# A two-layer sequence model on one core: half of the first input projection cut along its contraction and set between the loads of the first modulation

## The chip, the core and the metric

The kernel runs as one program on one core of a Trainium2 chip. The core has five engines with their own instruction streams: TensorE (PE: matmuls, and PEld: the loading of the stationary operand), VectorE (DVE), ScalarE (ACT), GpSimd (POOL) and SyncE (SP, which here only issues DMA transfers). They wait for each other through semaphores. All data are float32. The metric is the time of one execution on the device in microseconds, less is better. The kernel before takes 3230.65 us, the median of three runs from 3228.79 to 3232.77.

## The reference, cut to what matters

Two blocks with 256 tokens of width 2048 are computed one after the other. The change touches only the very start of the first block, its first layer:

```
c_act = silu(c)                                         # one vector of 2048
shift, scale, gate = split(c_act @ mod_w[0] + mod_b[0])  # 2048 x 6144
h = rmsnorm(x, norm_g[0]) * (1 + scale) + shift          # 256 x 2048
u, z = split(h @ w_in, 2)                                # 2048 x 4096, u and z 256 x 2048 each
dt = exp(log_step); a = exp(lam * dt)                    # the state space model's constants
bb = coefficient(a, lam) * b
x = scan(a, u * bb); y = gelu(Re(c * x) + d * u)          # the S5 scan along the 256 tokens
y = y * sigmoid(y @ w_glu + b_glu)
out = (y * silu(z)) @ w_out
```

After it come a sparse attention layer and a whole second model; nothing of their work is changed.

## The kernel before, in words

Weights stream from HBM in tiles of 2 MB. A tile is 128 partitions by 4096 floats: 16 chunks (`j`) along the contraction by 256 output columns. Four such tiles have room on the chip at once, in `ring`, whose four slots are filled in turn: tile number n lies in slot n % 4. SP issues the loads strictly in order, and `load` (L208 to L211) waits with each until its slot has been handed back (`slot_free`). One DMA queue carries all of them. Activations lie transposed, width on the partitions: `xT` and `hT` hold 16 chunks by 256 tokens, 2 MB each.

The start runs in these steps:

- SP loads the constants, `xT` and the raw state space matrices, then the 16 tiles of `mod0` (shift and scale of the first layer), then small parameters, then the tiles of `u`, among which are mixed the tiles for later modulations (`stream_mixed`).
- DVE computes the constants of the state space model (`dve_ssm_params`, `dve_ssm_matrices`: 18 large operations on 128x2048 floats), and then waits for the modulation.
- For each of the 16 tiles of `mod0`, PE multiplies the vector `c_act` with the tile (`mod_rows`, L388), ACT copies the resulting row to `ROW_STAGE` and hands the slot back (L972), and PE turns the row into columns (`mod_row_columns`, L394), one tile later, while the next tile's rows are done. From the ninth tile on, PE also does two blocks of transposes per tile for the state space model (`pe_transposed`, L1145 and L1150), and ACT copies them away.
- When all 32 columns are there, DVE adds the bias and forms `hT` in four quarters of 4 chunks each (`dve_norm0`, L979 to L993), and signals `h_ready` after each.
- PE does the first input projection `u` (`dense`, L280): eight tiles of 256 output columns, each 2 x 16 matmuls of 128x128 by 128x256. The profile counts each float32 matmul as two records, so a tile has 64. ACT drains each tile's bank into `u_all` (L414).
- Beside it DVE forms four pairs of modulation tiles (`mod_pair`, L348 and L350: one pair of tiles, weighted by `c_act` and summed over the 16 chunks), and PE sums each over the partitions (`mod_columns`, L365).
- Then comes the scan (`pe_ssm`, `dve_ssm`, `act_ssm`, `pool_ssm`), 16 blocks, with the tiles of `z` worked off between them.

The order of the instructions on each engine is written out by hand; there is no scheduler. Every engine takes its stream in order.

## Time and profile before

| | us |
|---|---|
| three runs, median | 3230.65 |
| the profiled execution's own time | 3228.36 |
| span in its profile | 3226.6 |
| PE busy in the span | 3142.2 (97%) |
| first rows of the first modulation tile, start | 26.47 |
| last rows of the sixteenth, start | 101.20 |
| first matmul of `u`, start | 110.06 |
| last `mod_columns` beside `u`, end | 226.8 |

The profile is of one execution. Its times count from the span's start. A chain of waits goes back from the last instruction to what released each step. A stretch's row gives each engine's busy time in it, and the granted clock of PE (1.00 is 2.4 GHz, 0.50 is 1.2 GHz). PE is busy nearly all the time, but not in the first 120 us, and that is where the change lies.

### The profile page before, as it was taken

What the parts mean: (1) busy time and instruction counts of PE and PEld (TensorE: products, weight loads), DVE (VectorE), ACT (ScalarE), POOL (GpSimd) and SP (SyncE); (2) the same over time, 40 slices, a digit from 0 to 9 for tenths busy, and PEclk for the clock granted to TensorE, in tenths of its full rate; (3) what the DMA queues carried; (4) which work ended last, traced back from release to release, by engine and by line L of the source; (5) the groups of instructions that cost most, each with busy time, mean ns of one, the idle gap of its engine ahead of it and who ended that gap; (6) DMA issues with size and microseconds to landing.
All of it is one profiled execution on the core that took longest, in us unless ns stands there. A gap on an engine that the chain in (4) does not pass through costs nothing.

```text
span 3226.6 us, 54024 instructions
## 1 busy us (share of the span) xinstructions
PE 3142.2 (97%) x22938; PEld 2866.8 (89%) x22938; DVE 1730.4 (54%) x2645; ACT 454.2 (14%) x801; POOL 139.3 (4%) x89
## 2 busy tenths in 40 slices
PE   5899999989999999999999999999999999999999
PEld 3788888878889888898888888899999999999999
DVE  6448844444245243475636754567665655555443
ACT  2104510000001133312310012210000000000000
POOL 0004310000000000021000000000010000000000
PEclk8999999999999999999999999999999999999999
DMA  9873568766574323243344442324544444444443
GB/s 409 339 288 158 202 253 324 291 256 245 229 287 152 136 105 130 105 153 138 128 159 168 157 144 98 133 105 147 193 157 173 166 165 173 159 179 162 161 166 137
DMA packets 51017, 599.38 MB, mean 186 GB/s; under 512 B 9535, under 2 KB 12190, under 8 KB 13342
## 3 DMA queue, kind: packets, MB, share of 16 engines
q1 hardware_dynamic: 50846, 596.88, 48.0%
q8 instruction: 134, 2.20, 0.3%
q14 instruction: 37, 0.30, 0.0%
HBM read 593.70 MB, written 3.16 MB: 185 GB/s over the span
## 4 chain that ended last, share of the span: by engine, by line
PE 93%; DMA 3%; DVE 2%; DVEq 1%; ACT 0%; issue 0%; SPq 0%; POOLq 0%; POOL 0%; ACTq 0%
PE bank L2601 25%; PE bank L735 18%; PE bank L280 16%; PE bank L786 16%; PE bank L310 4%; DMA ring<-in_t_mod 3%; PE bank L732 2%; PE bank L322 2%; PE bank L561 1%; PE aux L1609 1%; PE bank L388 1%; PE bank L551 1%; PE aux L1656 1%; PE aux L1231 1%; PE bank L518 1%; PE bank L1249 0%
## 5 line engine op out<-in xcount | busy, mean ns | idle before, releaser
L735 PE MATMUL bank<-hT,ring 128*128 128x256 f32 x2496 | 552.5, 380 | 0.0
L735 PEld LDWEIGHTS bank<-hT,ring 128*128 128x128 f32 x2496 | 470.8, 190 | 76.6 <-issue 15.3
L2601 PE MATMUL bank<-arena,ring 128*128 128x128 f32 x3440 | 396.4, 275 | 0.0
L2601 PEld LDWEIGHTS bank<-arena,ring 128*128 128x128 f32 x3440 | 390.2, 192 | 0.0
L280 PE MATMUL bank<-arena,ring 128*128 128x256 f32 x1536 | 336.6, 381 | 8.3 <-DVE arena L635 5.7
L280 PEld LDWEIGHTS bank<-arena,ring 128*128 128x128 f32 x1536 | 292.2, 191 | 49.1 <-issue 6.0
L786 PE MATMUL bank<-hT,ring 128*128 128x128 f32 x2624 | 320.2, 277 | 7.7 <-DVEq L841 5.8
L786 PEld LDWEIGHTS bank<-hT,ring 128*128 128x128 f32 x2624 | 305.6, 193 | 13.2 <-issue 7.2
L280 PE MATMUL bank<-hT,ring 128*128 128x256 f32 x1024 | 224.9, 382 | 4.8 <-DVE hT L993 4.8
L280 PEld LDWEIGHTS bank<-hT,ring 128*128 128x128 f32 x1024 | 194.8, 191 | 32.2 <-issue 4.5
L2601 PE MATMUL bank<-hT,ring 128*128 128x128 f32 x1680 | 197.9, 275 | 0.0
L2601 PEld LDWEIGHTS bank<-hT,ring 128*128 128x128 f32 x1680 | 192.7, 192 | 0.1
L350 DVE SCALAR_TENSOR_TENSOR E<-ring,c_act,E 128x512 f32<-128x512 f32 x240 | 181.7, 757 | 19.0 <-issue 1.3
L786 PE MATMUL bank<-arena,ring 128*128 128x128 f32 x1472 | 175.6, 275 | 0.0
L786 PEld LDWEIGHTS bank<-arena,ring 128*128 128x128 f32 x1472 | 170.2, 192 | 0.4
L2692 DVE TENSOR_TENSOR arena<-bank,w_gate 128x256 f32<-128x256 f32 x50 | 21.2, 424 | 204.1 <-ACT rstd L2640 132.5
L2601 PE MATMUL bank<-arena,E 128*128 128x128 f32 x1024 | 119.7, 275 | 0.0
L2601 PEld LDWEIGHTS bank<-arena,E 128*128 128x128 f32 x1024 | 117.0, 192 | 0.0
L310 PE MATMUL bank<-hT,ring 128*128 128x256 f32 x512 | 116.0, 385 | 0.0
L310 PEld LDWEIGHTS bank<-hT,ring 128*128 128x128 f32 x512 | 96.8, 192 | 14.8 <-issue 0.4
L2098 DVE TENSOR_TENSOR W<-E,arena 128x128 f32<-128x128 f32 (+7 forms) x64 | 74.8, 1169 | 46.7 <-issue 29.6
L1676 DVE TENSOR_TENSOR arena<-aux,con 128x60 f32<-128x60 f32 (+2 forms) x24 | 17.1, 712 | 129.7 <-PE aux L1609 129.7
(438 smaller groups left out, 3639.6 us busy)
## 6 DMA issues: line engine op xcount, KB each, us to landing
ring<-in_t_mod SPq DMA_DIRECT2D x64, 2048.0 KB, 13.4
ring<-in_t_gu SPq DMA_DIRECT2D x44, 2048.0 KB, 8.2
ring<-in_t_out SPq DMA_DIRECT2D x16, 2048.0 KB, 8.3
ring<-in_t_zs SPq DMA_DIRECT2D x16, 2048.0 KB, 8.3
ring<-in_t_down SPq DMA_DIRECT2D x16, 2048.0 KB, 7.4
ring<-in_t_gdn SPq DMA_DIRECT2D x12, 2048.0 KB, 8.2
ring<-in_t_u SPq DMA_DIRECT2D x8, 2048.0 KB, 10.3
ring<-in_t_z SPq DMA_DIRECT2D x8, 2048.0 KB, 9.1
```

Of the source, the lines that this page charges most:

```text
L280: last = nc.tensor.matmul(bank[s][:, T * f:T * f + T], w[:, j, P * f:P * f + P], act[:, j, :], start=j == 0, stop=j == kd - 1)
L310: last = nc.tensor.matmul(bank[s][:, T * f:T * f + T], w[:, j, P * f:P * f + P], act[:, j, :], start=j == 0, stop=j == KD - 1)
L322: last = nc.tensor.matmul(bank[s][:, T * f:T * f + T], act[:, j, P * f:P * f + P], w[:, j, :], start=j == 0, stop=j == KD - 1)
L350: nc.vector.scalar_tensor_tensor(a, w, c_act[:, j:j + 1], a, ALU.mult, ALU.add)
L388: last = nc.tensor.matmul(out[32 * q:32 * q + 32, :], c_act[:, j:j + 1].to_broadcast([P, 32]), w[:, j, :], start=a == 0, stop=a == KD // 4 ...
L518: last = nc.tensor.matmul(out[:, T * f:T * f + T], w[:, j, P * f:P * f + P], act[:, j, :], start=m == 0, stop=m == 2 * KD - 1)
L551: last = nc.tensor.matmul(out[:, T * f:T * f + T], w[:, j, P * f:P * f + P], x[:, j, :], start=j == 0 and f == 0, stop=j == KD - 1 and f == 1)
L732: last = nc.tensor.matmul(out[:, T * f:T * f + T], act[:, j, P * f:P * f + P], w[:, j, :], start=j == 0, stop=j == kd - 1)
L735: last = nc.tensor.matmul(out[:, T * f:T * f + T], w[:, j, P * f:P * f + P], act[:, j, :], start=j == 0, stop=j == kd - 1)
L786: last = nc.tensor.matmul(out[:, P * at:P * at + P], a[:, j, :], tile_at(b, j), start=j == 0 and q in (0, 3), stop=j == half - 1 and q in ...
L2098: v.tensor_tensor(tmp, Tsol[:, :, 0:J], row, ALU.mult)
L2601: last = nc.tensor.matmul(out[:, P * q:P * q + P], a[:, j, :], b[:, j, :], start=begins and q == 0 and j == 0, stop=ends and q == len(grou ...
```

## The change

The projection `u` (2048 columns out of 2048) is cut in two halves of 1024 output columns.

The first half is cut along the contraction: four tiles `uk`, each with 4 chunks of the contraction (one quarter of `hT`) by 1024 output columns, again 2 MB. They take places in the stream of `mod0`, which is reordered: after four modulation tiles that give shift and scale of one quarter comes that quarter's `uk` tile. So `mod0` has 20 tiles. PE works each off in `pe_u_slice` (32 matmuls, into four banks that are kept open over all four slices), after `h_ready` for its quarter. DVE forms `hT` quarter by quarter as the columns come: the first quarter in the midst of `dve_ssm_matrices`, the others behind it. The transposes for the state space model move into the second and third slice, one block of them after each group of four matmuls, and through one bank of `aux` in place of two banks. `mod_rows` now writes to `aux`, and the columns of a tile follow its rows at once, after ACT's copy.

The second half is done as before in four tiles of 256 columns (`pe_u_rest`), but the weights go to two side rooms in place of ring slots: `arena[:, 4096:8192]`, free when the transposes are done (`k0_ready`), and `xT`, free when `hT` is complete. The pairs of modulation tiles have the ring alone: pair 0 in slots 0 and 1, pair 1 in 2 and 3, and so on. For that the raw matrices lie in the arena and no longer in `hT`, a rounding buffer of the scan lies in `w_gate`, and `w_gate` itself is loaded after the scan, ahead of the second load of `xT`.

```
-ORDER = [("mod0", 16), ("u", 16), ("z", 16), ("glu", 16), ("out", 16), ("kv", 16), ("kvrow", 4),
+ORDER = [("mod0", 20), ("u", 8), ("z", 16), ("glu", 16), ("out", 16), ("kv", 16), ("kvrow", 4),
...
+        def mod0_slot(m):
+
+            q, x = m // QUARTER, m % QUARTER
+            return 5 * q + x, 8 * (x // 2) + 2 * q + x % 2
+
+        def whole(name, k):
+            return (lambda slot: slot[:, 0:SLOT]), t["t_" + name][k]
+
+        def stream_mod0(sp):
+            for q in range(4):
+                for m in range(QUARTER * q, QUARTER * q + QUARTER):
+                    n, tile = mod0_slot(m)
+                    load(sp, n, 0, whole("mod", tile))
+                load(sp, 5 * q + 4, 0, whole("uk", q))
+
+        U_ROOMS = [arena[:, 4096:8192], xT[:].rearrange("p j n -> p (j n)")]
+        u_in = [sem(f"u_in{q}") for q in range(2)]
+        u_drained = sem("u_drained")
+
+        def sp_u_rest(sp):
+
+            def dense_load(m):
+                if m == 0:
+                    sp.wait_ge(k0_ready, 1)
+                elif m == 1:
+                    sp.wait_ge(h_ready, 4)
+                else:
+                    sp.wait_ge(products, 4 + m - 1)
+                sp.dma_start(U_ROOMS[m % 2], t["t_u"][m]).then_inc(u_in[m % 2], 16)
+
+            def pair_load(p):
+                for x, (n, r) in enumerate(mod_slots("u", p // 2, p % 2)):
+                    load(sp, n, r, whole("mod", 2 * PAIRS["u"] + 2 * p + x))
+
+            dense_load(0)
+            pair_load(0)
+            dense_load(1)
+            pair_load(1)
+            for p in (2, 3):
+                dense_load(p)
+                pair_load(p)
...
+        def pe_u_slice(pe, q):
+
+            n = 5 * q + 4
+            wait_landed(pe, n, 0)
+            pe.wait_ge(h_ready, q + 1)
+            w = ring[:, n % RING, :].rearrange("p (j n) -> p j n", j=QUARTER)
+            for o in range(8):
+                for j in range(QUARTER):
+                    last = nc.tensor.matmul(bank[o // 2][:, T * (o % 2):T * (o % 2) + T], w[:, j, P * o:P * o + P],
+                                            hT[:, QUARTER * q + j, :], start=q == 0 and j == 0 and o % 2 == 0,
+                                            stop=q == 3 and j == QUARTER - 1 and o % 2 == 1)
+                if q == 3 and o % 2:
+                    last.then_inc(products, 1)
+                elif q < 3 and o == 7:
+                    last.then_inc(slot_free[n % RING], 1)
+                if q in TURNED:
+                    pe_transposed(pe, 8 * TURNED.index(q) + o)
+
+        def pe_u_rest(pe):
+            for m in range(4):
+                pe.wait_ge(u_in[m % 2], 16 * (m // 2 + 1))
+                pe.wait_ge(u_drained, m + 1)
+                w = U_ROOMS[m % 2].rearrange("p (j n) -> p j n", n=SLOT_COLS)
+                for f in range(2):
+                    for j in range(KD):
+                        last = nc.tensor.matmul(bank[m][:, T * f:T * f + T], w[:, j, P * f:P * f + P], hT[:, j, :],
+                                                start=j == 0, stop=j == KD - 1)
+                last.then_inc(products, 1)
+                if m:
+                    mod_columns(pe, "u", (m - 1) // 2, (m - 1) % 2)
+            mod_columns(pe, "u", 1, 1)
+
+        def act_u(act, first):
+            for m in range(first, first + 4):
+                act.wait_ge(products, m + 1)
+                if m == 3:
+                    act.nop().then_inc(slot_free[(BASE["u"] - 1) % RING], 1)
+                act.wait_ge(params_in, 16 * N_PARAMS)
+                nc.scalar.activation(u_all[:, 2 * m:2 * m + 2, :], bank[m % 4][:].rearrange("p (f n) -> p f n", f=2),
+                                     ACT.Copy).then_inc(u_drained, 1)
...
-            for n in range(COUNT["mod0"]):
-                if n > 1:
-                    wait_free(pe, n + RING - 2, 0)
-                wait_landed(pe, n, 0)
-                mod_rows(n, bank[n % 2][:, 0:SLOT_COLS])
-                if n:
-                    wait_free(pe, n + RING - 1, 0)
-                    mod_row_columns(ROW_STAGE[(n - 1) % 2], A(1, 2 * n - 2, 2))
-                if n >= FIRST_TURNED:
-                    for b in range(2):
-                        pe_transposed(pe, 2 * (n - FIRST_TURNED) + b)
-            wait_free(pe, n + RING, 0)
-            mod_row_columns(ROW_STAGE[n % 2], A(1, 2 * n, 2))
+
+            def columns(m):
+                n, tile = mod0_slot(m)
+                wait_free(pe, n + RING, 0)
+                mod_row_columns(ROW_STAGE[m % 2], A(1, 2 * tile, 2))
+
+            for q in range(4):
+                for m in range(QUARTER * q, QUARTER * q + QUARTER):
+                    n, _ = mod0_slot(m)
+                    wait_landed(pe, n, 0)
+                    mod_rows(n, MOD_ROWS)
+                    columns(m)
+                pe_u_slice(pe, q)
 
             pe.wait_ge(bT_kept, SBLOCKS)
 
         def act_mod0(act):
...
+            for q in range(4):
+                for m in range(QUARTER * q, QUARTER * q + QUARTER):
+                    if m > 1:
+                        act.wait_ge(cols_ready, m - 1)
+                    act.wait_ge(rows_ready_m, m + 1)
+                    nc.scalar.copy(ROW_STAGE[m % 2], MOD_ROWS).then_inc(slot_free[mod0_slot(m)[0] % RING], 1)
+                if q in TURNED:
+                    for b in range(8):
+                        act_transposed(act, 8 * TURNED.index(q) + b)
...
+        def dve_norm0(dve, q):
+
+            first = QUARTER * q
+            at = slice(first, first + QUARTER)
+            dve.wait_ge(cols_ready, QUARTER * q + QUARTER)
+            nc.vector.tensor_tensor(SH0[:, at], A(1, first, QUARTER), col("mod_b", first, QUARTER), ALU.add)
+            nc.vector.tensor_tensor(SC0[:, at], A(1, 16 + first, QUARTER), col("mod_b", 16 + first, QUARTER), ALU.add)
+            dve.drain()
...
+            nc.vector.tensor_tensor(h4[:, at], x4[:, at], r4, ALU.mult)
+            dve.drain()
+            for j in range(first, first + QUARTER):
+                last = nc.vector.tensor_scalar(hT[:, j, :], hT[:, j, :], gain[:, j:j + 1], SH0[:, j:j + 1],
+                                               ALU.mult, ALU.add)
+            last.then_inc(h_ready, 1)
             dve.drain()
...
-        RAW_RE, RAW_IM = hflat[:, 0:2048], hflat[:, 2048:4096]
+        RAW_RE, RAW_IM = B(3, 0, 2048), B(3, 2048, 2048)
...
-        ROUNDED = MS[:, 0:512]
+        ROUNDED = w_gate[:].rearrange("p j n -> p (j n)")[:, 0:512]
...
             scaled(BB[0], BB[1], RAW_RE, RAW_IM, t6, t7)
-            scaled(BB[2], BB[3], RAW_RE, RAW_IM, c_re, c_im)
+            dve_rstd(dve, 0)
+            scaled(BB[2], BB[3], RAW_RE, RAW_IM, c_re, c_im, lambda: dve_norm0(dve, 0))
             v.nop().then_inc(bb_ready, 1)
             scaled(CA_RE, CA_IM, C_RE, C_IM, t3, t2)
...
-                last = nc.tensor.transpose(bank[2 + b % 2][:, P * m:P * m + P], BB[m][:, at], ident)
+                last = nc.tensor.transpose(A(0, P * m, P), BB[m][:, at], ident)
...
-            stream_mod0(sp, mod_tiles)
+            stream_mod0(sp)
             sp_params(sp)
-            for name in ("u", "z", "glu"):
+            sp_u_rest(sp)
+            for name in ("z", "glu"):
                 stream_mixed(sp, name, tiles_of(name), mod_tiles)
             sp.wait_ge(y_kept, SBLOCKS)
+            sp.dma_start(w_gate[:].rearrange("p j n -> p (j n)"), t["w_gate"]).then_inc(x_again, 16)
...
-            dense(pe, "u", hT, ready=(h_ready, 0, QUARTER))
+            pe_u_rest(pe)
...
+            act_u(act, 0)
             act_trig(act, 0)
-            drain_to(act, "u", u_all)
+            act_u(act, 4)
...
-            dve_rstd(dve, 0)
+            for q in (1, 2):
+                dve_norm0(dve, q)
             dve_k0(dve)
-            dve_mod0_bias(dve)
-            dve_norm0(dve)
+            dve_norm0(dve, 3)
             dve_turns(dve, 0)
             dve_mods(dve, "u")
...
+        "uk": x["ssm_w_in"][0][:, 0:D // 2].reshape(4, 4, P, D // 2).transpose(0, 2, 1, 3).reshape(4, P, -1),
```

PE at the second slice: before, each tile's rows (L388) and the columns of the tile before (L394) were followed by two blocks of transposes (L1145, L1150).

```order
L388 MATMUL bank<-ring,c_act 32x256 x16
L394 MATMUL aux<-sel,W 128x1 x2
L1145 MATMUL bank<-con,arena 128x128 x4
L1150 MATMUL aux<-arena 32x32 x8
L1145 MATMUL bank<-con,arena 128x128 x4
L1150 MATMUL aux<-arena 32x32 x8
L388 MATMUL bank<-ring,c_act 32x256 x16
L394 MATMUL aux<-sel,W 128x1 x2
```

The same place in the changed kernel: L470 and L476 are rows and columns, L343 the slice's matmuls, L1229 and L1234 the transposes; the waits in brackets are those of a row's first instruction.

```order
L470 MATMUL aux<-ring,c_act 32x256 [waits weights_in0]
L470 MATMUL aux<-ring,c_act 32x256 x15
L476 MATMUL aux<-sel,W 128x1 [waits slot_free0]
L476 MATMUL aux<-sel,W 128x1
L343 MATMUL bank<-hT,ring 128x256 [waits h_ready,weights_in1]
L343 MATMUL bank<-hT,ring 128x256 x3
L1229 MATMUL aux<-con,arena 128x128 [waits bT_kept,bb_ready]
L1229 MATMUL aux<-con,arena 128x128 x3
L1234 MATMUL aux<-arena 32x32 x8
L343 MATMUL bank<-hT,ring 128x256 x4
```

A slice stands in PE's stream behind the fourth tile's columns and ahead of all rows of the next quarter, and waits for `h_ready`.

SP's queue from the first weight tile on, in the changed kernel, with the slot that each load waits for:

```order
L211 DMA ring<-in_t_mod 128x4096 [waits slot_free3]
L211 DMA ring<-in_t_uk 128x4096 [waits slot_free0]
L211 DMA ring<-in_t_mod 128x4096 [waits slot_free1]
L211 DMA ring<-in_t_mod 128x4096 [waits slot_free2]
L211 DMA ring<-in_t_mod 128x4096 [waits slot_free3]
L211 DMA ring<-in_t_mod 128x4096 [waits slot_free0]
L211 DMA ring<-in_t_uk 128x4096 [waits slot_free1]
```

The fourth modulation tile behind a `uk` tile takes the slot in which that `uk` tile lay. Later in the same queue the loads for the second half of `u` (L245) and the pairs (L211) alternate:

```order
L245 DMA arena<-in_t_u 128x4096 [waits products]
L211 DMA ring<-in_t_mod 128x4096 [waits slot_free0]
L211 DMA ring<-in_t_mod 128x4096 [waits slot_free1]
L245 DMA xT<-in_t_u 128x4096 [waits products]
L211 DMA ring<-in_t_mod 128x4096 [waits slot_free2]
L211 DMA ring<-in_t_mod 128x4096 [waits slot_free3]
```

Before, each of these two `u` tiles waited for a slot of the ring; now it waits for the matmuls that last read its side room, and the pair stands behind it.

## Rows read from the trace of the kernel before

**Rows 1.** The profile page's head: span, and busy time of each engine (share, instructions).

```profile
span 3226.6 us, 54024 instructions
PE 3142.2 (97%) x22938; PEld 2866.8 (89%) x22938; DVE 1730.4 (54%) x2645; ACT 454.2 (14%) x801; POOL 139.3 (4%) x89
```

**Rows 2.** Stretches: from:to, length, busy us by engine, PEclk, DMA share, GB/s.

```profile
51.00:105.80 54.80, 42.92 (x724) 29.29 (x723) 14.49 (x8) 13.88 (x29) 0.00 (x0) 0.96 1.00 420
105.80:226.80 121.00, 116.15 (x545) 101.81 (x544) 60.20 (x89) 8.33 (x13) 3.80 (x3) 0.99 0.76 307
```

**Rows 3.** Waits of SP's queue up to 105 us: total us, times, longest.

```profile
SPq L211 <- ACT W L972: 84.5, 16, 20.4
```

**Rows 4.** The chain of waits up to 440 us: start, us, what.

```profile
84.16 16.90 DMA ring<-in_t_mod
...
155.06 27.73 PE bank L280 x128
...
226.02 0.80 PE aux L365 x8
```

**Rows 5.** PE in order of time: start, us, line, operation, records, idle before.

```profile
42.38 3.64 PE L388 MATMUL bank<-ring,c_act 128*32 128x256 f32 x32 [3.25 <-DMA ring<-in_t_mod]
45.96 1.02 PE L394 MATMUL aux<-sel,W 128*128 128x1 f32 x4
...
81.58 1.93 PE L388 MATMUL bank<-ring,c_act 128*32 128x256 f32 x32 [0.81 <-DMA ring<-in_t_mod]
...
101.20 1.93 PE L388 MATMUL bank<-ring,c_act 128*32 128x256 f32 x32 [0.87 <-DMA ring<-in_t_mod]
103.06 0.61 PE L394 MATMUL aux<-sel,W 128*128 128x1 f32 x4
103.53 0.63 PE L1145 MATMUL bank<-con,arena 128*128 128x128 f32 x4
...
105.20 0.61 PE L394 MATMUL aux<-sel,W 128*128 128x1 f32 x4
110.06 7.09 PE L280 MATMUL bank<-hT,ring 128*128 128x256 f32 x24 [4.25 <-DVE hT L993]
...
231.46 2.09 PE L1231 MATMUL aux<-arena 32*128 32x128 f32 x32 [3.09 <-DVE xT L1306]
233.47 8.35 PE L310 MATMUL bank<-hT,ring 128*128 128x256 f32 x32
```

**Rows 6.** ACT in order of time, the copy that frees a slot.

```profile
83.62 0.37 ACT L972 COPY W<-bank 128x256 f32<-128x256 f32 x1 [2.50 <-PE bank L388]
```

**Rows 7.** DVE in order of time: norm of the first quarter, and the last pair.

```profile
40.20 2.29 DVE L1124 TENSOR_TENSOR arena<-hT,small 128x2048 f32<-128x2048 f32 x1
...
63.58 1.75 DVE L621 RECIPROCAL rstd<-rstd 128x256 f32<-128x256 f32 x1
...
106.87 0.19 DVE L979 TENSOR_TENSOR mod<-aux,cols 128x32 f32<-128x32 f32 x1
...
108.53 1.38 DVE L993 TENSOR_SCALAR hT<-hT,gain,mod 128x256 f32<-128x256 f32 x4
...
203.54 0.48 DVE L348 TENSOR_SCALAR E<-ring,c_act 128x512 f32<-128x512 f32 x1 [15.15 <-DMA ring<-in_t_mod]
...
214.12 2.40 DVE L350 SCALAR_TENSOR_TENSOR E<-ring,c_act,E 128x512 f32<-128x512 f32 x3 [0.20 <-issue]
```

**Rows 8.** DMA issues at 155.2 and at 184.0 us, queue empty: us to landing last.

```profile
ring<-in_t_u SPq DMA_DIRECT2D x1, 2048.0 KB, 8.1
...
ring<-in_t_u SPq DMA_DIRECT2D x1, 2048.0 KB, 8.7
```

**Rows 9.** Stretches as in rows 2, for the granted clock.

```profile
42.00:51.00 9.00, 8.47 (x70) 4.46 (x70) 8.65 (x5) 0.49 (x2) 0.00 (x0) 0.50 1.01 431
...
110.00:113.00 3.00, 2.94 (x7) 2.42 (x8) 2.92 (x6) 0.00 (x0) 0.00 (x0) 0.50 1.00 426
...
229.00:235.00 6.00, 3.54 (x36) 3.05 (x37) 5.78 (x8) 2.35 (x4) 1.53 (x1) 0.51 0.90 347
```

More of the change, by code:

```diff
@@ L83 @@
 MIXED = ("u", "z", "glu", "out", "kv", "q")
-DENSE = {n: 0 if n == "mod0" else c // 2 if n in MIXED else c for n, c in ORDER}
+DENSE = {n: 0 if n == "mod0" else 8 if n == "u" else c // 2 if n in MIXED else c for n, c in ORDER}
 PBASE = {n: sum(DENSE[m] for m, _ in ORDER[:k]) for k, (n, _) in enumerate(ORDER)}
@@ L259, in mod_slots @@
         def mod_slots(name, i, k):
+            if name == "u":
+                return [(BASE[name] + 2 * k + x, i) for x in range(2)]
             return [(BASE[name] + 4 * k + (2 - x if name == "q" else 1 + x), 2 * i) for x in range(2)]
@@ L921, in sp_params @@
         def sp_params(sp):
-            for dst, src in ((w_gate[:].rearrange("p j n -> p (j n)"), t["w_gate"]),
-                             (w_beta[:].rearrange("p j n -> p (j n)"), t["w_beta"]),
+            for dst, src in ((w_beta[:].rearrange("p j n -> p (j n)"), t["w_beta"]),
                              (cmp_w2[:], t["cmp_w2"].rearrange("k a b -> a k b")),
@@ L965, in pe_mod0 @@
             pe.wait_ge(bT_kept, SBLOCKS)
         def act_mod0(act):
-            for n in range(COUNT["mod0"]):
-                if n > 1:
-                    act.wait_ge(cols_ready, n - 1)
-                act.wait_ge(rows_ready_m, n + 1)
-                nc.scalar.copy(ROW_STAGE[n % 2], bank[n % 2][:, 0:SLOT_COLS]).then_inc(slot_free[n % RING], 1)
-                if n >= FIRST_TURNED:
-                    for b in range(2):
-                        act_transposed(act, 2 * (n - FIRST_TURNED) + b)
@@ L980, in dve_mod0_bias @@
+        def dve_norm0(dve, q):
[4 more added lines that the diff above has]
+            nc.vector.tensor_tensor(SC0[:, at], A(1, 16 + first, QUARTER), col("mod_b", 16 + first, QUARTER), ALU.add)
             dve.drain()
[L982 to L984 removed]
+            nc.vector.scalar_tensor_tensor(gain[:, at], SC0[:, at], 1.0, col("norm_g", first, QUARTER), ALU.add, ALU.mult)
@@ L987, in dve_norm0 @@
             r4 = rstd[:].rearrange("p (o c s) -> p o s c", o=1, s=2).to_broadcast([P, QUARTER, 2, P])
-            for q in range(4):
-                at = slice(QUARTER * q, QUARTER * q + QUARTER)
-                nc.vector.tensor_tensor(h4[:, at], x4[:, at], r4, ALU.mult)
-                dve.drain()
-                for j in range(QUARTER * q, QUARTER * q + QUARTER):
-                    last = nc.vector.tensor_scalar(hT[:, j, :], hT[:, j, :], gain[:, j:j + 1], SH0[:, j:j + 1],
-                                                   ALU.mult, ALU.add)
-                last.then_inc(h_ready, 1)
+            nc.vector.tensor_tensor(h4[:, at], x4[:, at], r4, ALU.mult)
[4 more added lines that the diff above has]
+            last.then_inc(h_ready, 1)
             dve.drain()
         u_all, z_all = tiles(B(0)), tiles(B(1))
-        hflat = hT[:].rearrange("p j n -> p (j n)")
         xflat = xT[:].rearrange("p j n -> p (j n)")
-        RAW_RE, RAW_IM = hflat[:, 0:2048], hflat[:, 2048:4096]
+        RAW_RE, RAW_IM = B(3, 0, 2048), B(3, 2048, 2048)
         BB = [arena[:, 2048 * k:2048 * k + 2048] for k in range(4)]
@@ L1115, in dve_ssm_matrices, with scaled @@
             v = nc.vector
-            def scaled(re, im, x_re, x_im, a_re, a_im):
+            def scaled(re, im, x_re, x_im, a_re, a_im, between=None):
                 def g(x):
@@ L1125, in scaled @@
                 dve.drain()
+                if between:
+                    between()
                 v.tensor_tensor(re, re, tmp, ALU.subtract)
@@ L1156, in act_transposed @@
             act.wait_ge(bT_ready, b + 1)
-            nc.scalar.copy(BT[:, b, :], bank[2 + b % 2][:]).then_inc(bT_kept, 1)
+            nc.scalar.copy(BT[:, b, :], A(0)).then_inc(bT_kept, 1)
         def dve_k0(dve):
```

34 lines of the change are left out of this document (13 added, 21 removed).

## The prediction, made before the changed kernel was run

> **What bounds the kernel now.** I read the page's head first: PE is busy for 97% of the 3226.6 us span [rows 1], so nearly everywhere a change gains only what it takes off PE. Then the stretches of the start, where PE has gaps. From tile 4's rows at about 51 us to PE's first pause after the modulation (105.80) it is busy 42.92 of 54.80 us, with the DMA engines full (share 1.00, 420 GB/s); from there to the end of the u stage (226.80) it is busy 116.15 of 121.00 us [rows 2]. All idle time there is to win is thus 11.9 + 4.8 = 16.7 us. Third, the waits of SP's queue: 84.5 us, all on ACT's copies, which hand the slots back [rows 3]. The chain of waits up to there is a row of DMA pieces such as the 16.90 us at 84.16 [rows 4], and the rows on PE start every (101.20 - 81.58)/4 = 4.9 us [rows 5]: one 2 MB tile per 4.9 us. That is a full queue with three transfers outstanding; it depends on each slot coming back within a few us. After 110 us the chain is PE's own.
>
> So the stretch before 105.8 is bound by DMA and the one behind it by PE. The change puts PE work into the first. What it is worth depends on whether the loads keep running meanwhile.
>
> **The ring.** They don't. A `uk` slice holds one of four slots until its 32 matmuls are done, and the fourth modulation tile behind it needs that slot. PE has to work off the slice before it touches the next tiles, and the next slice needs all four of them. With the slice at 13.87 us (27.73/2, 64 records [rows 4]) the queue runs dry in each quarter: three tiles take 15 us to land, and then SP waits. The stretch stops being bound by DMA and becomes one serial chain on PE, with DVE's norm in it.
>
> **The chain, piece by piece.** It starts with tile 3, whose loads nothing has changed: rows at 42.38, 3.64 us at the half clock that the trace grants there [rows 5, 9], ACT's copy (0.37, with 0.1 to either side), columns about 1.0 (the half-clock row at 45.96): 47.6. DVE is free: the norm comes behind the third operation of the second `scaled`, which ended at 42.5 and now has the reciprocal of 1.75 ahead of it, so 44.3 [rows 7]. Norm of one quarter: from the bias at 106.87 to the fourth `L993` at 109.91, and PE started at 110.06, so 3.2; a second small add and the semaphore make it 3.4. First slice at 51.0.
>
> From there, in PE's order:
> - four slices, 4 x 13.87 = 55.5, and four tiles of the second half, again 55.5. The order of the matmuls over banks changes, their number and shape don't; I take the same duration.
> - 16 blocks of transposes: two take 103.53 to 105.20, so 0.84 each, 13.4. ACT's copy of a block lies beside the next four matmuls (1.73 us), so the single bank costs nothing; without that cover it would be about 0.8 for each of 16.
> - 12 modulation tiles. Start to start, rows are 1.93 less 0.07 of overlap, columns 0.54 or so (103.06 against 103.53). Before, the columns of one tile ran in the wait for the next; now they follow the copy: 81.58 to the end of the copy at 83.99 [rows 5, 6] is 2.4, 0.1 for the semaphore, 0.5 for the columns: 3.0 each, 36.0.
> - three more norm waits, 3 x 3.4 = 10.2. DVE is free for each (the last large operation ended at 63.5, just ahead of the reciprocal at 63.58; with that, 3.3 of waiting and 3.4 of norm in front it ends near 72).
> - the clock. PE's pauses of 3.25, 4.25 and 3.09 us were each followed by work at 0.50 [rows 5, 9]. At 110.06, 24 records took 7.09 where 24 x 0.217 = 5.2: 1.9 lost. At 233.47, 32 records of the same shape took 8.35 for 6.9: 1.4 lost, beside what the 32 small ones ahead of them lost. The new pauses before slices are 3.4 us, so 4 x 2.0 = 8.0.
> - three `mod_columns`, 3 x 0.80 = 2.4 [rows 4].
>
> Sum 181.0; PE would be through at 232.0, and with the last `mod_columns` at 232.8. Before it was 226.02 + 0.80 = 226.8.
>
> The fourth modulation tile of a quarter must not come later than PE: its load is issued at the slice's end, lands 8.1 to 8.7 later [rows 8], and PE arrives after three tiles, 9.0. It is just hidden (with 0.8 more to spare where transposes follow the last group); if it weren't, every us counts three times.
>
> **The last pairs.** The loads of the second half wait for `products`, and the pairs stand behind them in SP's queue. The third of these tiles is issued when the first is worked off: 232.0 - 3 x 13.87 - 2.4 = 188.0. It lands after 8.4, and five more tiles (pair 2, the fourth tile, pair 3) follow without a gap, 5 x 4.9 = 24.5: pair 3 is there at 220.9. DVE takes 214.12 + 2.40 - 203.54 = 13.0 [rows 7], and PE's columns 0.9 with the semaphore: 234.8. That is 2.0 behind PE and is what the scan waits for. Shift: 234.8 - 226.8 = 8.0 us.
>
> The row says 8.1 to 8.7 for a lone 2 MB load [rows 8]. The Trainium skill (DMA: Bandwidth & Descriptors, "Anatomy of one DMA — SWDGE (gpsimd) path") gives, for another issuing path than SP's, 2.0 us plus the bytes at 436 GB/s, an estimate of 6.8 us; by it the pair would come 1.6 earlier and the shift would be 6.4. The trace does not agree, and I go by the row.
>
> **What else moves.** POOL and ACT start the scan's first sines after `h_ready` 4 (near 158), long before they are used; the small parameters are there by then. The first `z` tiles need slots 0 and 1, free when DVE is through with pair 2, near 219, and are hidden behind pair 3; the next two come free at 234 and are used 10 us into the scan or later. `w_gate` now goes ahead of the second `xT` load, 0.4 MB or 0.9 us at 420 GB/s, hidden behind the whole glu stage. The scan opens as before: PE's pause before its second inputs stays. Each of these I take at zero; the bound above is 0.9 for `w_gate`, and a late `z` tile would cost at most one load, 8.7.
>
> Own time of the profiled execution 3228.36 + 8.0 = 3236.4. That execution is 2.3 faster than the median of the runs, 3230.65, so the forecast is 3230.65 + 8.0 = 3238.7 us.
>
> **Bounds of the unknown terms.** Clock: nothing lost at all, to one slice wholly at half clock (13.9 more). Norm wait: 3.2 to 4.5. Copy between rows and columns: 2.9 to 3.2 per tile. Landing: 8.1 to the 10 or so of a queue with three tiles in it, on the fourth tiles 0 to 3 x 1. Own range of the forecast: 3233 to 3245.
>
> **Rivals.**
> 1. *The clock stays up.* For: after the slice PE is busy some 80%, more than at 42 or 62 us. Against: rows 5 and 9, three pauses, three drops. PE would be through at 224.8, the third tile issued at 180.0, and the pair route ends at 180.0 + 8.4 + 24.5 + 13.0 + 0.9 = 226.8: shift 0, 3230.7. The Trainium skill (TensorE: Matmul & The Clock Gate, "Part 1") says that the number of slow matmuls after a start differs from run to run, and that the whole penalty is small; the two rows that I can price, 1.9 and 1.4 or more, are of one size, so this keeps a modest chance.
> 2. *PE is filled after all (the other side).* Place: the pauses before the four slices and between rows and columns. If `hT`'s quarter were there when PE comes, and copies lay under other work, PE would only do its work: 55.5 + 55.5 + 13.4 + 12 x 2.4 + 3.2 = 156.4 from 51.0, through at 207.4: shift -19, 3211. It decides where the pause before a slice is under 1 us. Against: the norm reads the last columns, which PE makes just before the slice, and nothing else stands between them in PE's order. For it I have only that the profile doesn't show this order.
> 3. *The clock stays down over the tiles too.* A tile then costs 3.64 + 0.6 + 1.02 = 5.2 in place of 3.0; one quarter of four tiles adds 9: 3247.5. For: at 42 to 51 us PE did two tiles in a row at 0.50. Against: the tiles now follow a full slice.
> 4. *The change doesn't do what it says:* a side room's tile comes late and PE waits for it, one load of 8.7 more, 3247. Against: the first is issued near 147 and used near 174, the third has 13.9 us for 8.4.
>
> **Chances.** Forecast 0.60, rival 1 0.17, rival 2 0.08, rival 3 0.12, rival 4 0.03. The range reaches from below rival 1 to just past rival 3: 3229 to 3248. A change under 0.2% (6.5 us, 3224.2 to 3237.1) can't be told from none. The forecast lies 1.6 above that bound, I give 0.43 of its 0.60 to slower, 0.16 to same, 0.01 to faster; with rivals 3 and 4 slower is 0.58, with rival 1 same is 0.32, and faster, with rival 2 and what I may have missed, 0.10.
>
> **What would show it.** In the changed profile: first slice at about 51.0, the others near 82, 120 and 158; before each a pause of 3.4 us on PE put down to DVE's `hT`, and a granted clock near 0.5 in its first 3 us. GB/s falls to zero in each of the first three slices, and PE, not DMA, carries the chain from 51 us. PE's last `mod_columns` wait about 2 us for DVE and end near 235. From the scan on all is shifted, with the same lengths. I am wrong if the slices come closer than 30 us (rival 2), if their first matmuls run at full clock (rival 1), or if the modulation tiles behind a slice are more than 3.3 us apart (rival 3, or a late fourth tile).

## The result

The changed kernel takes 3239.86 us (median of 10 runs, 3237.82 to 3243.11) against 3230.87 (10 runs, 3228.79 to 3233.12) on the same chip: 9.0 us slower, ratio 1.0029 with a 95% interval of 1.002 to 1.0037. Forecast were 3238.7 us and a shift of 8.0. Its profiled execution took 3241.53 us.

The head of its page answers to [rows 1]. PE is busy for 10 us more, with the same number of PE instructions:

```profile
span 3239.8 us, 53917 instructions
PE 3152.4 (97%) x22938; PEld 2875.0 (89%) x22938; DVE 1731.8 (53%) x2655; ACT 454.0 (14%) x801; POOL 138.5 (4%) x89
```

The stretches as in [rows 2] (from:to, length, busy us of PE, PEld, DVE, ACT, POOL, clock, DMA share, GB/s), the second now to the last `mod_columns` beside u, then two that lie inside slices:

```profile
51.00:105.80 54.80, 48.83 (x461) 37.29 (x461) 20.80 (x16) 6.54 (x13) 0.00 (x0) 0.94 0.66 271
105.80:234.20 128.40, 115.58 (x832) 95.31 (x831) 55.31 (x84) 15.76 (x28) 3.49 (x3) 0.96 0.83 342
...
60.00:66.00 6.00, 6.00 (x38) 4.84 (x40) 5.85 (x4) 0.00 (x0) 0.00 (x0) 1.00 0.01 5
94.00:102.00 8.00, 8.00 (x86) 6.59 (x85) 0.00 (x0) 1.76 (x3) 0.00 (x0) 1.00 0.00 0
```

PE does more before 105.8 (48.83 us against 42.92), as was meant, but the second stretch has not become shorter (128.4 us against 121.0): it holds 12.8 idle us where it held 4.9, and a lower clock. The loads stand still in the middle of a slice. What SP's queue waits for, up to 235 us (total, times, longest), has answers to [rows 3] in its first two rows:

```profile
SPq L211 <- PE bank L343: 71.5, 3, 25.5
SPq L211 <- ACT W L1055: 61.7, 15, 22.4
```

L343 are the slices: three loads waited for them, 71.5 us. PE in order of time (start, us, line, records, idle before), answering to [rows 5]:

```profile
42.10 1.93 PE L470 MATMUL aux<-ring,c_act 128*32 128x256 f32 x32
44.58 0.61 PE L476 MATMUL aux<-sel,W 128*128 128x1 f32 x4 [0.55 <-ACT W L1055]
48.43 16.98 PE L343 MATMUL bank<-hT,ring 128*128 128x256 f32 x64 [3.25 <-DVE hT L1075]
65.34 1.94 PE L470 MATMUL aux<-ring,c_act 128*32 128x256 f32 x32
...
71.37 1.93 PE L470 MATMUL aux<-ring,c_act 128*32 128x256 f32 x32
73.86 0.61 PE L476 MATMUL aux<-sel,W 128*128 128x1 f32 x4 [0.55 <-ACT W L1055]
74.39 1.93 PE L470 MATMUL aux<-ring,c_act 128*32 128x256 f32 x32
...
80.72 2.83 PE L343 MATMUL bank<-hT,ring 128*128 128x256 f32 x8 [3.24 <-DVE hT L1075]
...
103.12 1.92 PE L470 MATMUL aux<-ring,c_act 128*32 128x256 f32 x32
...
118.47 3.03 PE L343 MATMUL bank<-hT,ring 128*128 128x256 f32 x8 [3.24 <-DVE hT L1075]
...
156.27 15.74 PE L343 MATMUL bank<-hT,ring 128*128 128x256 f32 x64 [3.25 <-DVE hT L1075]
171.84 13.98 PE L360 MATMUL bank<-hT,arena 128*128 128x256 f32 x64
...
232.27 1.87 PE L447 MATMUL aux<-ones,E 128*128 128x1 f32 x8 [2.44 <-DVEq L435]
```

Each slice stands behind an idle time of 3.25 us that ends with DVE's norm. The fourth tile of the second quarter (74.39), whose load had to wait for the slice, starts 3.02 us after the third with no idle time for a DMA: the starved load is just hidden. The clock at a slice's start answers to [rows 9]:

```profile
48.00:52.00 4.00, 3.57 (x9) 2.89 (x10) 3.83 (x3) 0.00 (x0) 0.00 (x0) 0.50 0.98 418
...
156.00:160.00 4.00, 3.73 (x10) 3.09 (x11) 0.55 (x2) 0.00 (x0) 2.31 (x2) 0.60 0.99 420
```

A slice at full clock takes 13.82 us: two undisturbed tiles of the second half, which have as many records each, took 27.64 in the chain below. The first slice took 16.91 (to the rows at 65.34) and the last 15.57 (to the tile at 171.84). The two with transposes took 22.40 (80.72 to 103.12) and 22.43. Their undisturbed groups of eight records and one block start 2.62 us apart, and the last group takes 2.5, so at full clock such a slice is 7 x 2.62 + 2.5 = 20.85. Lost are thus 3.1, 1.55, 1.6 and 1.75 us in the order of the slices, 8.0 together. The expectations below took 21.0 for a slice with transposes, and so 7.7.

The end of the u stage is DVE's. Its last pair, answering to [rows 7] (L430 and L432 are L348 and L350 of before), and the chain of waits there:

```profile
219.31 0.48 DVE L430 TENSOR_SCALAR E<-ring,c_act 128x512 f32<-128x512 f32 x1 [2.59 <-DMA ring<-in_t_mod]
219.87 12.31 DVE L432 SCALAR_TENSOR_TENSOR E<-ring,c_act,E 128x512 f32<-128x512 f32 x15
```

```profile
172.00 27.64 PE bank L360 x128
...
200.51 18.67 DMA ring<-in_t_mod
...
232.27 1.88 PE aux L447 x8
234.52 2.13 PE aux L1315 x32
```

The last columns end at 234.1, 7.3 us later than before; the scan's opening adds 1.3, and the scan ends at 426.46 against 417.81 in these two executions. That is 8.65 us, against 9.0 between the medians. The two profiles differ by 13.2 us in the span. Of the other 4.55 us, 3.5 arise in the glu stage: the changed kernel's execution waited 2.6 us for a tile, the one before 2.1, and then it did 128 records in 30.88 us, the one before in 27.89. This loss does not go with the change: the same 128 records took 27.89 in the traces of e1 and e12, which contain the change, and 29.58 in e9, which is the kernel before with extra matmuls.

### The profile page after: what moved, and what is told of

It reads as the page before. It is cut to its first block, busy times and chain, and to the rows that moved or that the text cites. A ratio compares the mean times of both kernels' runs of the same rounds, so it can differ in the third digit from the quotient of the medians.

```text
span 3239.8 us, 53917 instructions
## 1 busy us (share of the span) xinstructions
PE 3152.4 (97%) x22938; PEld 2875.0 (89%) x22938; DVE 1731.8 (53%) x2655; ACT 454.0 (14%) x801; POOL 138.5 (4%) x89
## 4 chain that ended last, share of the span: by engine, by line
PE 94%; DMA 2%; DVE 2%; DVEq 1%; ACT 1%; issue 0%; SPq 0%; POOLq 0%; POOL 0%; ACTq 0%
PE bank L2683 25%; PE bank L817 18%; PE bank L868 16%; PE bank L321 13%; PE bank L392 4%; PE bank L343 2%; PE bank L814 2%; PE bank L404 2%; DMA ring<-in_t_mod 2%; PE aux L470 1%; PE bank L360 1%; PE bank L643 1%; PE aux L1693 1%; PE bank L633 1%; PE aux L1740 1%; PE aux L1315 1%
## 5 line engine op out<-in xcount | busy, mean ns | idle before, releaser
L817 PE MATMUL bank<-hT,ring 128*128 128x256 f32 x2496 | 552.5, 380 | 0.0
L817 PEld LDWEIGHTS bank<-hT,ring 128*128 128x128 f32 x2496 | 471.4, 190 | 76.0 <-issue 15.3
L868 PEld LDWEIGHTS bank<-hT,ring 128*128 128x128 f32 x2624 | 307.1, 194 | 13.4 <-issue 7.2
L2683 PEld LDWEIGHTS bank<-hT,ring 128*128 128x128 f32 x1680 | 192.8, 192 | 0.1
L432 DVE SCALAR_TENSOR_TENSOR E<-ring,c_act,E 128x512 f32<-128x512 f32 x240 | 181.0, 754 | 18.0
L392 PE MATMUL bank<-hT,ring 128*128 128x256 f32 x512 | 116.9, 387 | 0.0
L321 PE MATMUL bank<-hT,ring 128*128 128x256 f32 x512 | 111.5, 380 | 0.0
L392 PEld LDWEIGHTS bank<-hT,ring 128*128 128x128 f32 x512 | 97.6, 193 | 15.0 <-issue 0.4
L321 PEld LDWEIGHTS bank<-hT,ring 128*128 128x128 f32 x512 | 97.1, 190 | 13.1 <-issue 0.2
```

Of the source, the lines that this page charges most:

```text
L321: last = nc.tensor.matmul(bank[s][:, T * f:T * f + T], w[:, j, P * f:P * f + P], act[:, j, :], start=j == 0, stop=j == kd - 1)
L392: last = nc.tensor.matmul(bank[s][:, T * f:T * f + T], w[:, j, P * f:P * f + P], act[:, j, :], start=j == 0, stop=j == KD - 1)
L432: nc.vector.scalar_tensor_tensor(a, w, c_act[:, j:j + 1], a, ALU.mult, ALU.add)
L817: last = nc.tensor.matmul(out[:, T * f:T * f + T], w[:, j, P * f:P * f + P], act[:, j, :], start=j == 0, stop=j == kd - 1)
L868: last = nc.tensor.matmul(out[:, P * at:P * at + P], a[:, j, :], tile_at(b, j), start=j == 0 and q in (0, 3), stop=j == half - 1 and q in ...
L2683: last = nc.tensor.matmul(out[:, P * q:P * q + P], a[:, j, :], b[:, j, :], start=begins and q == 0 and j == 0, stop=ends and q == len(grou ...
```

## The experiments

Each was timed in five rounds with the kernel before on the same chip. Differences are between medians. The ratio is a second estimate from the same runs, and the two can lie 1 us apart (e12: -7.7 by medians, -6.8 by the ratio). An interval of 0.1% to either side is 3 us, so differences of 1 or 2 us between two variants are not told apart by these times; where a trace shows them, that is said.

| kernel | difference, us | ratio (95%) | expected |
|---|---|---|---|
| changed | +9.0 | 1.0029 (1.002 to 1.0037) | +8.0 |
| e1_warm | +5.2 | 1.002 (1.0011 to 1.0029) | +1.3 |
| e3_half_pairs | +5.7 | 1.0018 (1.0009 to 1.0027) | +5 |
| e4_chunks | +3.4 | 1.0011 (1.0002 to 1.002) | +1 |
| e5_warm_first | +1.3 | 1.0003 (0.9994 to 1.0012) | +1.3 to +4.4 |
| e6_rooms | +9.5 | 1.0029 (1.0018 to 1.0041) | +9.0 |
| e7_before_warm | +0.3 | 1.0002 (0.9993 to 1.0011) | -4 |
| e8_chunks_warm | -3.2 | 0.999 (0.9981 to 0.9999) | -1.8 |
| e9_before_warm_first | -1.6 | 0.9997 (0.9988 to 1.0006) | -3.7 |
| e10_pairs_first | -4.1 | 0.999 (0.9982 to 0.9999) | -4.5 |
| e11_turned_in_pauses | -6.3 | 0.9984 (0.9975 to 0.9993) | -9 |
| e12_order_kept | -7.7 | 0.9979 (0.997 to 0.9988) | -7 |

The variant e2_late_columns, which turned each row into columns one tile later, gave no time; more on it below.

**e1_warm and e5_warm_first: the clock.**

```
             wait_landed(pe, n, 0)                 # e5: behind the added lines
+            for _ in range(7):                    # e5: 4 in the first quarter
+                nc.tensor.matmul(A(0, 0, T), ident, con[:, 0:T], start=True, stop=True)
             pe.wait_ge(h_ready, q + 1)
```

> The changed kernel with seven extra matmuls (128x128 by 128x256, on constants, into a bank that nobody reads) on PE in each of the four pauses between a quarter's last columns and its slice: 7 x 0.433 = 3.0 us in a pause of 3.24 us. Nothing else moves. Theory (one serial chain on PE, of which the half clock after the four pauses is 7.7 us: 16.91 for the first slice in place of 13.82, 22.4 in place of 21.0 for the second and third, 15.57 in place of 13.82 for the last): each slice runs at full clock from its first matmul, the last mod_columns end 7.7 us earlier, and the kernel is 1.3 us slower than the one before (3232), not 9. Rival A (the loads bind, the ring of four slots is what costs): the fourth tile of a quarter then arrives late, and of the 7.7 us at most 2 are seen: 3238. Rival B (the clock drops for another reason than the pause): the slices stay as long as they were, 3240.

> As e1_warm, but with the extra matmuls ahead of the wait for the uk tile, not behind it, since in e1_warm they began 0.9 to 1.8 us late and ran 1.0 to 1.8 us past the norm: seven of them (3.0 us) in the pauses of the second to fourth quarter, four in the first. They end before the norm does, so the slices start as in the changed kernel. Theory (serial PE chain; the half clock after the pauses costs it 1.4 + 1.45 + 1.75 us in the last three quarters, and about half of 3.1 in the first): slices start 32.0, 36.4 and 36.4 us apart from the second quarter on, and the shift against the kernel before falls from 9.0 by 4.6 to 7.7: 3225 + what the chip of the day adds, or 1.3 to 4.4 us above before. Rival (the uk tile lands too late: 1.4, 2.2 us and less ahead of the norm in the changed kernel): a wait for DMA in place of DVE ahead of the slices, and 6 us or more above before.

In e1 the extra matmuls waited for the `uk` tile and then ran past the norm. PE of e1, ahead of the first and second slice:

```profile
47.05 4.98 PE L344 MATMUL aux<-con 128*128 128x256 f32 x14 [1.82 <-DMA ring<-in_t_uk]
51.86 13.98 PE L349 MATMUL bank<-hT,ring 128*128 128x256 f32 x64
...
79.36 3.29 PE L344 MATMUL aux<-con 128*128 128x256 f32 x14 [1.47 <-DMA ring<-in_t_uk]
82.49 1.89 PE L349 MATMUL bank<-hT,ring 128*128 128x256 f32 x8
```

The slices ran at full clock (13.98) but started late, and 3.8 us of the gain are left. e5 mended that:

```profile
48.69 14.05 PE L349 MATMUL bank<-hT,ring 128*128 128x256 f32 x64 [1.42 <-DVE hT L1081]
...
74.67 3.27 PE L343 MATMUL aux<-con 128*128 128x256 f32 x14
78.06 1.97 PE L349 MATMUL bank<-hT,ring 128*128 128x256 f32 x8
```

Slices now start 29.4, 36.2 and 36.2 us apart (32.3, 37.8 and 37.8 in the changed kernel), and those with transposes take 20.8. The last columns end at 226.5, 7.6 us earlier. By the medians the kernel fell from 9.0 to 1.3 above before, 7.7 us; the 8.0 read off the slices agree. That the half clock after the pauses costs this is shown.

**e6_rooms: the ring.**

```
+                if q < 2:     # the slot goes on at once; the uk tile has a room of its own
+                    load(sp, 5 * q + 4, 0, ((lambda slot: slot[:, 0:16]), t["t_mod"][0][:, 0:16]))
+                    sp.wait_ge(bb_ready if q else ms_ready, 1)
+                    sp.dma_start(B(2 + q), t["t_uk"][q]).then_inc(uk_in, 16)
```

> The changed kernel with the first two uk tiles in rooms of their own, arena[8192:12288] and arena[12288:16384], which are free then; the ring's slot that each had is handed on at once (a load of 16 columns in its place). So in the first two quarters no modulation tile waits for a slice to be worked off, the loads run on during them, and the ring has all four slots. Theory (by the time of the slices the chain is serial on PE and DVE, the starved loads were just hidden: the fourth tile's rows never waited): no change, within 0.7 us of the changed kernel's 9.0 above before. Rival (the ring's starvation is what costs the 9 us): the stretch becomes bound by DMA again, and the kernel falls by 6 us or more, to 3 above before or less.

The loads did run on, 395 GB/s during the first slice against 274 in the changed kernel; the stretches of e6 and then of the changed kernel:

```profile
48.00:66.00 18.00, 17.45 (x83) 14.46 (x86) 17.48 (x10) 0.00 (x0) 0.00 (x0) 0.84 0.93 395
```

```profile
48.00:66.00 18.00, 17.57 (x76) 14.62 (x80) 17.48 (x9) 0.00 (x0) 0.00 (x0) 0.82 0.65 274
```

The time is the same, 9.5 above before (5.8 to 13 by the interval, where the rival wanted 3 or less). The trace says it more sharply: the slices start at 48.55, 80.48, 118.32 and 156.20, within 0.25 us of the changed kernel's 48.43, 80.72, 118.47 and 156.27. The starvation of the ring is real and costs nothing of itself; PE's and DVE's serial chain does. This is shown for the first two of the four slices; the other two kept their slot of the ring.

**e3_half_pairs: the last pair.**

```
-            for j in range(KD):
+            kd = KD // 2 if name == "u" else KD
+            for j in range(kd):
```

> The changed kernel with DVE's sums for the four pairs beside u taken over 8 of the 16 chunks (half of that modulation's product is left out): 6.5 us of DVE work less per pair. Theory (the last pair, not PE's own work, ends the u stage: PE stood idle for 2.44 us for it): PE does the last columns right behind those of pair 2, at 229.7 in place of 234.1; half of that from the pause, the rest because those columns and the first inputs of the scan run at full clock: 3239.9 - 4.0 = 3236 (between 2.4 and 5). Rival (PE's chain alone sets the end, and the pair is hidden): 3239.9, no change beyond 0.5 us.

The kernel leaves out half of the chunks in these sums. 3.3 us went by the medians, of 4.0. In its trace the columns of pairs 2 and 3 stand together, in one row of PE:

```profile
230.74 1.84 PE L448 MATMUL aux<-ones,E 128*128 128x1 f32 x16
```

From the last slice's start to the end of these it took 74.5 us, in the changed kernel 77.9.

**e4_chunks: the norm wait.**

```
-            for o in range(8):
-                for j in range(QUARTER):
+            for j in range(QUARTER):
+                pe.wait_ge(...)           # this chunk of hT
+                for o in range(8):
```

> The changed kernel with the matmuls of a slice in another order: chunk by chunk, each over all eight output tiles, with DVE signalling each of the four chunks; transposes stay two per chunk. A slice can start when its first chunk is there, three operations of 0.33 to 0.41 us sooner: the pause shrinks from 3.24 to 2.2 us, four times, 4.2 us. Theory (the norm wait is on the path): at least 4.2 us, 3235.7, and if a pause of 2.2 us no longer brings the clock down, up to 7.7 more, 3228. Before the change one pause of 2.42 us was followed by full clock and one by half, so I expect about half of that: 3232. Rival (the loads bind): at most 2 us, 3238.

5.6 us went, and the pauses are 2.28 us. The clock came back at once in one slice of four (the third: 1.96 us for its first 8 records), in the others not:

```profile
49.73 15.74 PE L347 MATMUL bank<-hT,ring 128*128 128x256 f32 x64 [2.28 <-DVE hT L1079]
79.82 2.96 PE L347 MATMUL bank<-hT,ring 128*128 128x256 f32 x8 [2.28 <-DVE hT L1079]
...
116.62 1.96 PE L347 MATMUL bank<-hT,ring 128*128 128x256 f32 x8 [2.28 <-DVE hT L1079]
...
151.85 15.74 PE L347 MATMUL bank<-hT,ring 128*128 128x256 f32 x64 [2.28 <-DVE hT L1079]
```

So 4 x 0.97 = 3.9 us of pause, and the remaining 1.7 are put down to the clock, mostly the third slice's. My "about half" of the 7.7 was too much.

**e7_before_warm and e9_before_warm_first: the same remedy in the kernel before.**

```
             pe_mod0(pe)
+            for _ in range(9):            # e7: inside dense, behind the wait for u's first tile
+                nc.tensor.matmul(A(0, 0, T), ident, con[:, 0:T], start=True, stop=True)
             dense(pe, "u", hT, ready=(h_ready, 0, QUARTER))
...
+                    if b == 0:            # the scan's pause, in both
+                        for _ in range(6):
+                            nc.tensor.matmul(bank[3][:, 0:T], ident, con[:, 0:T], start=True, stop=True)
                     inputs(b + 1)
```

> The kernel before with extra matmuls on PE in its own two pauses of this stretch: nine (3.9 us) in the 4.25 us ahead of the first matmul of u, six (2.6 us) in the 3.09 us ahead of the scan's second inputs. Theory (half clock after a pause is a cost on PE's path in both kernels): 1.9 us after the first pause and 2.2 us or more after the second are gone, 4 us (0.12%) below before, and both stretches stand at 1.00 in the granted clock. Rival (the clock comes back as late as before, or what is gained is waited for elsewhere): no change.

> As e7_before_warm, but the nine extra matmuls of the first pause stand ahead of the wait for u's first tile: in e7 they waited for it until 109.1, ran at half clock and pushed u back by 5.6 us, which ate the scan's gain of 1.8. Theory (half clock after a pause costs the kernel before 1.9 us ahead of u and 1.8 in the scan's opening): 3.7 us below before. Rival (a pause filled early doesn't keep the clock up for u): 1.8 below.

e7 repeated e1's mistake (u began at 115.7). e9 did not, u ran at full clock from its first matmul, and still its trace reaches the scan's end only 1.64 us earlier (416.17 against 417.81), all of it from the scan's opening. By the times alone its 1.6 us can't be told from none.

```profile
105.81 4.15 PE L2804 MATMUL aux<-con 128*128 128x256 f32 x18
110.18 1.97 PE L280 MATMUL bank<-hT,ring 128*128 128x256 f32 x8 [0.22 <-DVE hT L993]
112.68 1.99 PE L280 MATMUL bank<-hT,ring 128*128 128x256 f32 x8 [0.54 <-DVE hT L993]
115.28 1.99 PE L280 MATMUL bank<-hT,ring 128*128 128x256 f32 x8 [0.60 <-DVE hT L993]
117.87 36.53 PE L280 MATMUL bank<-hT,ring 128*128 128x256 f32 x168 [0.60 <-DVE hT L993]
```

PE waits here for each quarter of the norm, 2.6 us apart, and is through the fourth wait at 117.87, before at 117.75. The half clock at 110 was hidden by the norm; I had read it as 1.9 us lost [rows 5].

**e8, e10, e11, e12: towards a faster kernel.** e8 is e4 with extra matmuls in all pauses. e10 and e11 change this:

```
-            dense_load(0)        # e10 and e11: pair 0, tile 0, tile 1, pair 1, pair 2, tile 2, tile 3, pair 3
-            pair_load(0)         # e12: this order again
...
+            else:                # e11, e12: two blocks in each later pause, five in slices 2 and 3
+                for b in range(7 * q - 7, 7 * q - 5):
+                    pe_transposed(pe, b)
             wait_landed(pe, n, 0)
```

> e4_chunks with extra matmuls ahead of the slices (three in the first pause, five in the others, 2.2 us in 2.28) and six in the scan's pause. e4_chunks was 3.4 us above before. Theory: half clock after pauses costs it 1.7 + 1.3 + 0 + 1.75 in the slices and 2.2 in the scan. The uk tile now lands about when the first chunk does, so the waits go over to DMA: of the 5 us in slices 3 are seen, and 2.2 in the scan: 1.8 us below before (range 0 to 3.5 below). Rival (the uk tiles' landing takes all of it back): only the scan's 2.2: 1.2 above before.

> e8_chunks_warm (3.2 us below before) with the loads of the second half in the order pair 0, tile 0, tile 1, pair 1, pair 2, tile 2, tile 3, pair 3, and two extra matmuls in PE's pause ahead of the last mod_columns. Theory (DVE's pairs run in a chain, and the pause of 2.3 us there is the end of it: pair 3's load stands behind tile 3's): pair 0 starts 5 us earlier, pair 2 follows pair 1 without the wait of 4.3 us, pair 3 is then bound by its own landing 13 us after tile 3's issue; the pause shrinks by 1 to 1.5 us: 4.5 below before. Rival (PE waits for tile 2 now, since pair 2 is loaded ahead of it): no change against e8 or up to 3 us worse.

> e10 with six of the sixteen blocks of transposes taken out of the slices and put into the three later pauses, two each, in the place of the extra matmuls; the first pause keeps three extra matmuls. A block is 0.84 us of PE work; two blocks with the wait for ACT's copy of the first fit into the 2.28 us of the pause. Theory (serial PE chain): 6 x 0.84 = 5.0 us less on it, and the clock stays up as with the extra matmuls: 9 us below before (range 7 to 10). Rival (the uk tiles, which landed 0.3 us or less ahead of the norm in e4, now bind, since their slot comes free with a tile behind the slice before): a wait for DMA before the slices of 0.5 to 1.5 us each, 6 below before.

> e11 with the second half's loads again in the changed kernel's order (tile, pair, tile, pair ...), and four extra matmuls in PE's last pause, not two. In e10 and e11 PE waited 1.2 to 1.45 us for tile 0 and 0.65 to 1.06 for tile 2, and from the last slice to the last mod_columns e10 took 76.2 us where e8 took 75.3. Theory (PE's own chain and the pair's chain are within 2 us of each other, so the order of the loads only moves the wait): 1 us less than e11, 7 below before (range 5 to 9). Rival (the pairs bind): 1 to 2 us more than e11.

e8 gained 6.6 us on e4 by the medians and 4.6 in the two traces at the scan's end, where 5.2 was expected. That is right in sum, but by luck. No wait for the `uk` tiles came, so the slices and pauses gave 5.5 us in place of 3 (174.2 from the first slice's start to the last columns' end, 179.7 in e4). The scan's 2.2 did not come: its six extra matmuls ran at half clock, 4.84 us for 12 records, and put off the second inputs, so that 0.7 was lost there. e10 showed its rival: PE waited for the tiles of the second half instead. PE of e10 (tile 0, issued at 140.93, landed 20.7 us later, at 161.6, so the first wait is for it too):

```profile
161.70 14.05 PE L371 MATMUL bank<-hT,arena 128*128 128x256 f32 x64 [1.17 <-issue]
...
191.41 14.08 PE L371 MATMUL bank<-hT,arena 128*128 128x256 f32 x64 [1.06 <-DMA arena<-in_t_u]
```

Its 0.8 us on e8 lies within both intervals; from the first slice's start to the scan's end its trace has 364.4 us, e8's 365.6. In e11 slices 2 and 3 shrank, but two blocks with ACT's copy between them keep PE busy for only 1.8 of the 2.4 us, and the clock fell in two of the three pauses. e12, with the old order of loads, has the lowest difference: 7.7 us below before, 16.7 below the changed kernel. That it beats e11 is not shown, since their intervals overlap and its trace reaches the scan's end at 411.82, e11's at 411.31. Nor is it shown that the order of the loads helps: counted from the first slice's start e12 needs 362.7 us and e11 363.7, but e11 lost 1.6 in its last slice to the half clock, which e12's last slice did not. In e12 the clock fell after one of the three pauses. Its second slice and the pause ahead of it, then the start of the third slice:

```profile
75.08 0.64 PE L1241 MATMUL aux<-con,arena 128*128 128x128 f32 x4
75.65 0.33 PE L1246 MATMUL aux<-arena 128*32 128x32 f32 x16
76.48 0.63 PE L1241 MATMUL aux<-con,arena 128*128 128x128 f32 x4 [0.51 <-ACT arena L1253]
77.04 0.33 PE L1246 MATMUL aux<-arena 128*32 128x32 f32 x16
77.50 1.97 PE L354 MATMUL bank<-hT,ring 128*128 128x256 f32 x8
...
110.37 3.58 PE L354 MATMUL bank<-hT,ring 128*128 128x256 f32 x8
```

## Why the prediction was right

- *Bound and ring.* As said: after the first quarter nothing on PE waits for a modulation load, the queue is empty inside the first three slices, the chain is PE's and DVE's. e6 shows for the first two slices that the ring's starvation costs nothing on top.
- *First slice.* 51.0 forecast, 48.43 measured. Tile 3's rows, at half clock before, ran at full clock here: in this execution the clock came back during tile 2. In e3 and e4 the first slice began at 50.4 and, with a pause 1 us shorter, 49.7; the clock in these first 50 us differs from execution to execution.
- *Slices, tiles, pauses.* 13.87 us a slice: 13.82. 3.0 a modulation tile: 3.02. 3.4 a norm wait: 3.25. From the first slice's start to the last columns' end I had 183.8 us, it took 185.7.
- *Clock.* 8.0 forecast, 8.0 read off the slices, and 7.7 given back by e5. Right in sum, with some luck in its parts: forecast were 2.0 for each pause, measured 3.1 for the first and 1.55 to 1.75 for the others. Its price per pause was taken from rows of before of which the one at 110.06 stood under the norm (e9), so the number is right as the clock's own loss but would have been wrong as a cost of the kernel before.
- *The last pair.* 2.0 us behind PE forecast; measured were a pause of 2.44 and last columns at half clock (1.87 for 0.8), which I had left out, so that they end some 3.6 us later than PE alone would have had them. That is 1.6 of the 1.9 us that this path took longer than forecast. e3 gives the whole as 3.3. A lone load of a ring tile behind a slice (issued at 65.7) landed after 8.4 us, in the range of [rows 8]:

```profile
ring<-in_t_mod SPq DMA_DIRECT2D x1, 2048.0 KB, 8.4
```

- *The scan.* "As before" was 1.3 us short in these two executions: its opening stood at half clock for 6 us before and for 13 now. PE's pause for the pair comes just ahead of it, but that this is the cause is not shown. From the scan's first inputs to its first modulation rows it took 14.6 us before and 15.9 in the changed kernel, yet 14.3 in e4 and 14.4 in e5, which have the same pause; e6 has 15.8.
- *Sum.* The start was 2.6 us early, the path to the last columns 1.9 late and the scan 1.3; 8.0 against 8.65 in the traces and 9.0 in the medians. The mechanism was right; that the errors of the parts nearly cancel is luck.

The rivals: a clock that stays up would indeed have given a kernel within 0.2% of before (+1.3 in e5, forecast 0). Filling PE gave 16.7 us in e12, but by another order than the change's.

Not settled: the price of ACT's copy between rows and columns (0.55 us of PE idle per tile, 6.6 us in the twelve tiles of the later quarters) is read from the trace alone. e2_late_columns was written to take it away in three tiles of each quarter, with 5.2 us less than the changed kernel expected (2.5 or so if the loads bind). It gave no time: in it ACT read the bank of `aux` that PE was writing, with nothing to order the two. So of the idle time between 51 and 156 us this part stays unpriced. In e11 two of twelve executions took 4095 and 7058 us, and the table goes by the other ten; no other kernel here showed such times and the cause is open.

## What to carry to other kernels

Work pulled into a stretch that waits for loads must not make its own input the next thing to wait for: here every slice waited for a norm whose last input PE had just made, so a stretch bound by DMA became a serial chain, and its four pauses of 3.25 us cost 13 us and another 8 in the clock behind them. Ask of each new wait what the engine could do meanwhile that is independent: the transposes were there all along, and putting six of sixteen blocks into the pauses, with the matmuls turned so that the first chunk suffices, made the same split 7.7 us faster than the kernel without it. That kernel, e12, also has extra matmuls in the first pause, ahead of the last columns and in the scan's pause; the last of these brought the kernel without the split 1.6 us in its trace (e9). And before filling a pause for the clock's sake, look whether the slow matmuls behind it are themselves paced by another engine.

## What was not expected

Pauses of 2.28 us brought the clock down in three of four cases in e4. In e11 and e12 two blocks stood in such a pause, so that PE was busy for 1.8 of 2.4 us with one gap of 0.5 between the blocks, and still the clock fell in two of three cases and in one of three. Extra matmuls without a gap kept it up in all three later pauses of e5, e8 and e10. The Trainium skill (TensorE: Matmul & The Clock Gate, "HAM oscillation — how this bites in real kernels") tells of this with pauses of 3 to 5 us; these runs show it with shorter ones.
